# Up projections of a decoder trunk in fp32: four pairs of chunks by seven products instead of eight

## What is computed

```python
D_MODEL, SEQ, DEPTH, D_FF = 1024, 256, 2, 2816
def swiglu_ffn(h, w_in, w_out):
    g, u = jnp.split(h @ w_in, 2, axis=-1)
    return (jax.nn.silu(g) * u) @ w_out
for l in range(DEPTH):
    x = x + 0.5 * swiglu_ffn(rmsnorm(x, norm_ffn1[l]), ffn1_w_in[l], ffn1_w_out[l])
    ...      # four token mixers, then cross attention over mem
    x = x + 0.5 * swiglu_ffn(rmsnorm(x, norm_ffn2[l]), ffn2_w_in[l], ffn2_w_out[l])
return rmsnorm(x, norm_final)
```

## Time and profile before

| | |
|---|---|
| runs of before, median (three runs, 1096.26 to 1097.18) | 1097.18 us |
| the profiled execution, its own time | 1095.27 us |
| its span, first to last instruction | 1093.4 us |
| granted TensorE clock, mean | 0.999 |
| PE, PEld, DVE, ACT, POOL busy share | 99, 83, 75, 53, 36 % |
| hardware queue of SP: bytes, share of 16 engines | 200.55 MB, 55.4 % |

### The profile page before, as it was taken

How to read it: one execution, slowest core, us unless ns; L and a number is a source line. 1 busy time by engine, 2 the same in 40 slices (tenths; PEclk the granted TensorE clock), 3 DMA queues, 4 the chain that set the end, 5 groups by cost and what they waited for, 6 DMA issues and landing times.

```text
span 1093.4 us, 14359 instructions
## 1 busy us (share of the span) xinstructions
PE 1081.8 (99%) x5314; PEld 911.8 (83%) x5314; DVE 820.2 (75%) x1015; ACT 577.0 (53%) x656; POOL 391.8 (36%) x774
## 2 busy tenths in 40 slices
PE   8999999999999999999999999999999999999997
PEld 6888888889898888888878888788988988888886
DVE  6686798799767766668776667878997767666796
ACT  6454454854565544446454444567455555444544
POOL 0687722000000057673226868030000002677800
PEclk9999999999999999999999999999999999999999
DMA  8976557644553477655766764675445436666462
GB/s 277 294 246 215 167 192 256 210 155 149 197 194 116 147 219 225 210 186 182 259 214 209 229 209 150 220 249 193 154 169 187 177 123 197 217 216 217 144 222 107
DMA packets 180722, 215.94 MB, mean 197 GB/s; under 512 B 19088, under 2 KB 138540, under 8 KB 180652
## 3 DMA queue, kind: packets, MB, share of 16 engines
q1 hardware_dynamic: 155324, 200.55, 55.4%
q0 software_dynamic: 24064, 13.16, 4.4%
q10 hardware_dynamic: 1264, 1.32, 0.4%
HBM read 200.79 MB, written 1.05 MB: 185 GB/s over the span
## 4 chain that ended last, share of the span: by engine, by line
PE 88%; DVE 3%; DMA 3%; ACT 2%; issue 1%; POOL 1%; SPq 0%; ACTq 0%; DVEq 0%
PE acc L1640 24%; PE acc L1642 23%; PE acc L1641 23%; PE acc L1656 3%; PE acc L1657 3%; PE acc L1658 3%; PE turn L1517 2%; DMA w_raw<-in_ffn_w_out 2%; ACT w_hi L510 1%; POOL kT L463 1%; DVE w_lo L909 1%; DMA w_raw<-in_ffn_w_in 1%; PE acc L1582 1%; PE acc L1738 1%; PE acc L1737 1%
## 5 line engine op out<-in xcount | busy, mean ns | idle before, releaser
L909 DVE TENSOR_TENSOR w_lo<-w_raw,w_hi 128x2048 fp32r<-128x2048 f32 (+1 forms) x190 | 426.9, 2250 | 165.0 <-ACT w_hi L510 164.3
L510 ACT CAST w_hi<-w_raw 128x2048 fp32r<-128x2048 f32 (+1 forms) x190 | 356.2, 1875 | 195.2 <-PE acc L1642 135.1
L463 POOL DMA_DIRECT2D kT<-kT x704 | 344.3, 498 | 145.7 <-DVE kT L1057 106.8
L1640 PE MATMUL acc<-w_hi,xT 128*128 128x512 f32 x808 | 316.8, 392 | 0.0
L1642 PE MATMUL acc<-w_hi,xT 128*128 128x512 f32 x808 | 314.7, 389 | 0.0
L1641 PE MATMUL acc<-w_lo,xT 128*128 128x512 f32 x808 | 314.4, 389 | 0.0
L1642 PEld LDWEIGHTS acc<-w_hi,xT 128*128 128x128 f32 x808 | 151.7, 188 | 32.0
L1640 PEld LDWEIGHTS acc<-w_hi,xT 128*128 128x128 f32 x808 | 151.7, 188 | 31.1 <-DVE w_lo L909 0.4
L1641 PEld LDWEIGHTS acc<-w_lo,xT 128*128 128x128 f32 x808 | 151.8, 188 | 30.9
L1640 PE MATMUL acc<-w_hi,hT 128*128 128x512 f32 x432 | 170.3, 394 | 1.3 <-DVE w_lo L909 1.2
L1642 PE MATMUL acc<-w_hi,hT 128*128 128x512 f32 x432 | 168.4, 390 | 0.0
(11 more groups left out here) (218 smaller groups left out, 1228.4 us busy)
## 6 DMA issues: line engine op xcount, KB each, us to landing
w_raw<-in_ffn_w_in SPq DMA_DIRECT2D x172, 512.0 KB, 4.8
w_raw<-in_ffn_w_out SPq DMA_DIRECT2D x80, 512.0 KB, 4.4
w_raw<-in_mix_w_in SPq DMA_DIRECT2D x32, 512.0 KB, 4.7
w_raw<-in_xattn_wkv SPq DMA_DIRECT2D x32, 512.0 KB, 4.6
kT<-kT POOLq DMA_DIRECT2D x704, 16.0 KB, 3.4
w_raw<-in_mix_w_out SPq DMA_DIRECT2D x16, 512.0 KB, 4.1
w_raw<-in_xattn_wq SPq DMA_DIRECT2D x16, 512.0 KB, 4.5
w_raw<-in_xattn_wo SPq DMA_DIRECT2D x16, 512.0 KB, 4.3
```

The lines of the kernel that those rows point to most:

```text
L463: pool.dma_start(hfeat[B * q:B * q + B, g % 2, a * RUN:(a + 1) * RUN], hblk[B * a:B * a + B, g % 2, q * RUN:(q + 1) * RUN]).then_inc(hfeat ...
L510: act.copy(w_hi[:, u % SLOTS, 0:n], w_raw[:, u % SLOTS, 0:n]).then_inc(w_split_hi, 1)
L909: dve.tensor_tensor(w_lo[:, u % SLOTS, 0:n], w_raw[:, u % SLOTS, 0:n], w_hi[:, u % SLOTS, 0:n].bitcast(F32), ALU.subtract).then_inc(w_spli ...
L1640: pe.matmul(o, hi, wh, start=((first is True or first == ("tile", t)) and i == 0), stop=False)
```

## The change

In three of the four feed-forward parts (all but the first of layer 0), chunks 2+3, 4+5, 6+7 and 8+9 are computed as pairs. For feature tiles 0 and 1, the two token halves and the two chunks form a 2 x 2 by 2 x 2 block product, which was 8 products and becomes 7: one plain product into `acc` (m1), three of token sums by weight sums, one of a token sum by a plain tile, one of a plain token tile by a weight sum, and one more plain one. Partial results are passed on in PSUM: ScalarE copies m1 to a second bank (`m1_seed`), and copies that bank out twice while it grows (`u2_copy`, `u3_copy`); VectorE adds these copies into the banks of the second chunk (`m5_seed`, `u3_add`). The other 24 products of the pair stay as they are.

The pair's four units hold: u the tiles of features 0 and 1 for both chunks, u + 1 features 2 to 5 of the first chunk, u + 2 features 6 and 7 of both, u + 3 features 2 to 5 of the second. Units u and u + 2 are loaded by four transfers each in place of two. Of unit u only three of four tiles are split; the weight sums (`up_weight_sums`, three subtractions) and their split (`sums_hi`, `sums_lo`) are new. Token sums of features 0 and 1 are made once for each feed-forward part, ahead of `update`. The queues are reordered, and `hidden_hi(9)` in chunk 10 goes behind the second split in all four parts. `k_last` only moves to another place in SBUF.

```diff
+    UP_PAIRS = (2, 4, 6, 8)
+    def paired(l, f, c):
+        return (l, f) != (0, 0) and c in UP_PAIRS
...  ScalarE: split_hi
-                if e and e[0] == "singles":
+                if e and e[0] == "singles" or up_singles(at.l, u)[1]:
                     act.copy(w_hi[:, u % SLOTS, 0:GN], w_raw[:, u % SLOTS, 0:GN])
                     act.copy(w_hi[:, u % SLOTS, 2 * GN:n], w_raw[:, u % SLOTS, 2 * GN:n]).then_inc(w_split_hi, 1)
...  ScalarE: chunk(c)
                         act.activation(gate[:, t, :], acc[c % 3][t][:, 0:HC], ACT.Silu,
                                        scale=rstd[:, V_F2 if f else V_X, t:t + 1]).then_inc(gate_ready, 1)
+                        if t == 0 and paired(l, f, c + 1):
+                            m1_seed(c + 1)
                     if c >= 2:
                         hidden_hi(c - 2)
-                    split_hi(base + 2 * c + 4, at)
+                    if paired(l, f, c + 1):
+                        u2_copy(c + 1)
+                    if not paired(l, f, c) or not paired(l, f, c + 2):
+                        split_hi(base + 2 * c + 4, at)
+                    if paired(l, f, c + 1):
+                        u3_copy(c + 1)
+                    if c == 0 and (l, f) != (0, 0):
+                        up_token_hi()
+                        sums_hi(UP_PAIRS[0])
...
+                    split_hi(base + 2 * c + 5, at)
                     if c == FC - 1:
                         hidden_hi(c - 1)
-                    split_hi(base + 2 * c + 5, at)
+                    if paired(l, f, c + 1) and paired(l, f, c + 3):
+                        split_hi(base + 2 * (c + 3), at)
+                        sums_hi(c + 3)
+                def u3_copy(c):
+                    n = up_pair_no(l, f, c)
+                    act.wait_ge(m7_done, n + 1)
+                    act.copy(u3_sum, acc[c % 3][1][:, :]).then_inc(u3_copied, 1)
...  VectorE: chunk(c), behind the two hact
+                    if paired(l, f, c) and paired(l, f, c + 2):
+                        split_lo(base + 2 * (c + 2), at)
+                    if paired(l, f, c + 1):
+                        m5_seed(c + 1)
                     if c >= 2:
                         hidden_lo(c - 2)
+                    if paired(l, f, c) and paired(l, f, c + 2):
+                        sums_lo(c + 2)
...  behind the transpose
+                    if paired(l, f, c + 1):
+                        first_split()
+                        u3_add(c + 1)
+                        if paired(l, f, c + 3):
+                            up_weight_sums(base + 2 * (c + 3), at)
...  VectorE: ahead of update(b, 1, 0, ...) in boundary (f2in), and at the end of layer 0
+                    if g == G_FFN2:
+                        up_token_sums()
...  TensorE
+                def first_product(c):
+                    u = base + 2 * c
+                    pe.wait_ge(w_split, at0.at(UNITS, SLOTS + u + 1))
+                    plain(acc[c % 3][0][:, :], u, 0, 0, 0, first=True).then_inc(m1_done, 1)
+                def two_chunks(c):
+                    pe.wait_ge(us_ready, 2 * l + f)
+                    pe.wait_ge(ut_split, n + 1)
+                    summed(y1, 0, up_sum(0), first=True)
+                    pe.wait_ge(m1_seeded, n + 1)
+                    summed(x1, 2, up_sum(1)).then_inc(m6_done, 1)
+                    plain(x0, u, 2, 1, 0)
+                    pe.wait_ge(w_split, at0.at(UNITS, SLOTS + u + 2))
+                    plain(x0, u + 1, 0, 2, 0)
+                    pe.wait_ge(u2_copied, n + 1)
+                    summed(x1, 1, up_sum(2)).then_inc(m7_done, 1)
+                    plain(x0, u + 1, 1, 3, 0)
+                    plain(x0, u + 1, 2, 4, 0)
+                    pe.wait_ge(u3_copied, n + 1)
+                    summed(x1, 3, [xT_hi[:, 1, P:2 * P], xT_lo[:, 1, P:2 * P]])
+                    pe.wait_ge(m5_seeded, n + 1)
+                    into(y0, *up_sum(3), w_hi[:, u % SLOTS, 3 * GN:], w_lo[:, u % SLOTS, 3 * GN:]).then_inc(unit_done, 2)
+                    plain(x0, u + 1, 3, 5, 0).then_inc(unit_done, 1)
...
+                    # 4 products of u + 1, then unit u + 2: 4 into x0, x1 and 4 into y0, y1
+                    # (u3_added waited for ahead of y1), then unit u + 3: 4 into y0, the next
+                    # pair's first_product, 4 into y1
```

More of the change, by code:

```diff
@@ L69, in down, with up_singles @@
                 return f, DOWN[u - base]
+        return None, None
+    def up_singles(l, u):
+        for f, base in enumerate((U_F1I, U_F2I)):
+            if base <= u < base + 2 * FC and u % 2 == base % 2 and paired(l, f, (u - base) // 2):
+                return f, (u - base) // 2
         return None, None
@@ L386, in ffn @@
                 at = Layer(l)
+                f = 1 if base == U_F2I else 0
                 for c in range(FC):
+                    if paired(l, f, c):
+                        u = base + 2 * c
+                        pieces = two_chunk_parts(u, src_in, l, 0, c)
+                        unit(u, at, pieces[:2])
+                        for dst, src in pieces[2:]:
+                            sp.dma_start(dst, src).then_inc(second_k_landed, 16)
+                        unit(u + 1, at, pair_parts(u + 1, src_in, l, 2, c * HC, c * HC + FF))
+                        pieces = two_chunk_parts(u + 2, src_in, l, 6, c)
+                        unit(u + 2, at, pieces[:2])
+                        for dst, src in pieces[2:]:
+                            sp.dma_start(dst, src).then_inc(last_k_landed, 16)
+                        unit(u + 3, at, pair_parts(u + 3, src_in, l, 2, (c + 1) * HC, (c + 1) * HC + FF))
+                    if (l, f) != (0, 0) and (c in UP_PAIRS or c - 1 in UP_PAIRS):
+                        continue
                     for j in range(2):
@@ L1047, in first_split @@
                             extra(EXTRA[c])
-                    if c < FC - 1:
+                    if c < FC - 1 and not paired(l, f, c + 1) and not (paired(l, f, c) and paired(l, f, c + 2)):
                         first_split()
@@ L1154, in _ @@
                         xT_lo_part(0, 1, t, at)
[L1155 removed]
+                weights_to(2 if l else 3, at)
                 ffn(l, U_F1I, 0)
@@ L1712, in ffn, with into, plain @@
                 b = 3 if f else 0
+                def into(o, s_hi, s_lo, w_h, w_l, first=False, last=False):
+                    pe.matmul(o, s_hi, w_h, start=first, stop=False, skip_group_check=True)
+                    pe.matmul(o, s_hi, w_l, start=False, stop=False, skip_group_check=True)
+                    return pe.matmul(o, s_lo, w_h, start=False, stop=last, skip_group_check=True)
+                def plain(o, u, at_w, k, t, first=False, last=False):
+                    cols = slice(at_w * GN, (at_w + 1) * GN)
+                    rows = slice(t * P, (t + 1) * P)
+                    return into(o, xT_hi[:, k, rows], xT_lo[:, k, rows], w_hi[:, u % SLOTS, cols], w_lo[:, u % SLOTS, cols], first, last)
@@ new lines, in up_sum, with summed @@
+                def up_sum(i):
+                    return [us_parts[:, i // 2, q, (i % 2) * P:(i % 2 + 1) * P] for q in range(2)]
+                def summed(o, at_w, stationary, first=False):
+                    cols = slice(at_w * GN, (at_w + 1) * GN)
+                    return into(o, *stationary, t_hi[:, cols], t_lo[:, cols], first)
+                def first_product(c):
+                    u = base + 2 * c
+                    pe.wait_ge(w_split, at0.at(UNITS, SLOTS + u + 1))
+                    plain(acc[c % 3][0][:, :], u, 0, 0, 0, first=True).then_inc(m1_done, 1)
@@ L1720, in ffn @@
                 for c in range(1, FC):
+                    if (l, f) != (0, 0) and (c in UP_PAIRS or c - 1 in UP_PAIRS):
+                        if c in UP_PAIRS:
+                            two_chunks(c)
+                        continue
                     if (l, f, c) == (0, 0, 1):
@@ L1724, in ffn @@
                         unit(base + 2 * c, at0, c % 3, xT_hi, xT_lo, 0, True, False)
-                    unit(base + 2 * c + 1, at0, c % 3, xT_hi, xT_lo, GK, False, True)
+                    opens = (l, f) != (0, 0) and c == UP_PAIRS[0] - 1
+                    unit(base + 2 * c + 1, at0, c % 3, xT_hi, xT_lo, GK, False, True,
+                         between=lambda t: first_product(UP_PAIRS[0]) if opens and t == 0 else None)
                     if (l, f) == (0, 0) and c in EXTRA:
```

125 lines of the change are left out of this document (116 added, 9 removed).

## The result

| | before | changed |
|---|---|---|
| median of the runs on one chip | 1097.14 us | 1085.38 us (4 runs, 1084.46 to 1085.74) |
| ratio, 95% interval | | 0.9893 [0.9876, 0.9911] |
| the profiled execution, its own time | 1095.27 us | 1085.74 us |
| its span | 1093.4 us | 1083.9 us |
| granted clock | 0.999 | 0.999 |

The kernel became 11.8 us faster (1.1%), where 8.2 were forecast. In a later set it came to 1085.30 beside 1096.93: 11.6 us. The forecast of 1089.0 is 3.6 too high, and the range, from 1087.5, misses the time on its fast side.

A forecast was written before the change was run, and what follows sets the result against it. PE, busy 99%, was taken as the bound, time being the number of matmuls. -8.16 (products) + 0.94 (token sums) - 1.0 (order) + 0 (added waits) = -8.2 us, from 1097.18 to 1089.0 us; range 1087.5 to 1096.

The forecast's parts named there:

- The products: Up projections: one product of 32 removed in each of 12 pairs, 36 matmuls at 0.2267 us, -8.16 us.
- The relay: m6, copy, m7, copy on ScalarE in each pair: in time, cost 0, with 0.09 us spare at u3_copy.
- the price of a PSUM write: ScalarE's m1_seed taken at 0.59 us, VectorE's adds m5_seed and u3_add at 0.69; bounds 0.4 to 1.2.
- Rival 1: The relay of ScalarE copies in the pairs is late, 0.15 to 0.5 us each: 1091 to 1095, chance 0.25.
- The order: Down projections: hidden_hi(9) behind the second split shortens the split-load-split chain by 0.5 us; -1.0, bounds 0 and -1.5.
- the four waits: PE's waits for VectorE's splits in down projections: 1.2 us shown, about 2.1 us in cost.
- The step from one execution to the median: Whole kernel: the median of before stands 1.91 us over the profiled 1095.27, so -8.2 was taken from 1097.18.
- Token sums: Four 128x128 operations ahead of update: +0.94 us uncovered at the start of layer 1, bounds 0.8 and 1.3.
- VectorE's spare of 2.0 us a pair: VectorE busy 19.1 of 21.08 us; its next u + 1 split due T' + 1.8, T' starting the next pair's products.
- rival 2: VectorE becomes the bound in the pairs, needing 2.7 us more a pair to lose the saving: 1102.5, chance 0.10.
- Rival 3: The removed product turns up as PE waits, 0.5 to 0.7 us a pair: 1095 to 1098, chance 0.10.

The follow-up runs named there:

- the third set: Third set of follow-up timings on one chip, each kernel beside the kernel before: before 1096.93 us, changed kernel 1085.30 us.
- the repeated profile: The kernel before, unchanged, timed and profiled once more: 1096.72 us, ratio 1.0001; profiled execution 1097.38 us, span 1095.5.
- the order-only kernel: Kernel before with only hidden_hi(9) and hidden_lo(9) moved behind the second split: 1094.58 us, ratio 0.9976; later 1093.68, ratio 0.9973.
- the run with one addition: Changed kernel with one more VectorE addition of 1024 columns, result unused, behind sums_lo in every pair: 1093.32 us, ratio 0.9964.
- the old order: Changed kernel with hidden_hi(9) and hidden_lo(9) put back ahead of the second split: 1092.34 us, ratio 0.9957.
- six and nine pairs: Changed kernel with fewer pairs, UP_PAIRS (2, 4) or (2, 4, 6), in place of twelve: six 1091.66 us, nine 1088.10 us.

## Why the prediction missed

The direction and the main term were right, and three terms around it were not. Of the 3.4 us by which the third set (-11.6) went past the -8.2, 2.2 lie in the order (-3.25 against -1.0) and 1.2 in the pairs with their token sums (-8.4 against -7.2).

- **The products, -8.16: right.** 5278 matmuls, pairs 21.08 us apart, no wait in an up projection. By medians of one set the pairs brought 8.4 on top of the order.
- **The relay and the price of a PSUM write: right.** The seed from PSUM to PSUM took 0.57 us (0.59 was taken), VectorE's adds into PSUM 0.694 and 0.693 (0.69 was taken), the copies 0.589 and 0.586. Rival 1 (0.25) didn't happen; its spare of 0.09 measured 0.14.
- **The order, -1.0, bounds 0 and -1.5: the step that failed.** Alone it measured -2.6 and -3.0, and about -7 beside the pairs. The prediction worked out that the four waits cost 2.1 us, found that the moved split heads the chain on which they hang, and then took half of it. The gain on the chain was also sized at 0.5; it is 0.75 and later 1.13, and no wait shows more than 0.7. All of the 2.1 would have had to be taken, and the bound had to reach beyond it, to what a slower execution waits.
- **The step from one execution to the median: failed.** The prediction carried 1.91 us over as if it were fixed. It was for the most part waits of the very kind that the change removes: the repeated profile has 3.4 us of them, not 2.1, at a time 0.7 above its median. Some was the small sample: the medians of before in the three later sets are 0.2 to 0.7 lower than 1097.18. Changed, the profiled execution is 1085.74 and the median 1085.38; no offset is left. With the order at -2.1 the sum is -8.16 + 0.94 - 2.1 = -9.3, and 1095.27 - 9.3 = 1086.0; without the 1.91 on top that is the time within 0.6. That sum is made with the result known.
- **Token sums, +0.94: too high.** Moving them away from the one place that waits brought 0.8 us by the medians of one set and 0.6 by its spans. Part of even that is the wait that the order-only kernel has there without them (0.2 and 0.5).
- **VectorE's spare of 2.0 us a pair (rival 2): wrong, unseen in this kernel.** The down projection's token sums of chunks 0 to 2, which VectorE adds inside `hidden_lo` in the pairs (four operations, 0.93 us), were left out of the count: ahead of the second and third pair of a part the split ends at T' + 1.71, 0.1 ahead of its due time, where 0.8 were thought. Ahead of the fourth, without them, it ends at T' + 0.8, near the T' + 1.0 that was placed (631.37 + 2.25 against T' = 632.84). And rival 2 was said to decide at 2.7 us more a pair, with VectorE's idle time as a buffer; the run with one addition shows that it starts to cost at 0.1 in half of the pairs. The forecast stood because nothing in this kernel came late, not for the reason given.
- **Rival 3** (the product turns up as waits) happened only in the old order, where half of the gain was eaten.

Summed over the third set: -3.25 for the order, -8.4 for the pairs, -11.6 measured; -8.16 for the products and -3.4 for the waits make -11.6 too. But the 3.4 are those of an execution above the median, and the token sums' 0.6 to 0.8 are not in it: the account closes to about 1 us, no better, which is also what the waits drift by between executions and versions. What stays open is why the wait ahead of layer 1 is 1.2 and 1.0 us with six and nine pairs. Which share the two pieces of the new order, ScalarE's and VectorE's, have was not tried.

## What to carry to other kernels

If a change takes away the operation that heads a chain on which waits hang, charge all the waits and bound the gain by them at their full price (the row's idle time plus the part of the matmul that its row hides), and look at several executions, since a profile is one draw: where before differs between runs by waits that the change removes, the difference goes with them. Ask for the spare of a hand-over along the loop from engine to engine and back, in operations between the two signals; VectorE, at 91% of a pair or less by the prediction's count, had 0.1 us to spare in half of them. And time parts of a change both alone and together: here one reordering was worth about 3 us by itself and 7 beside the other half.

## What the runs showed of the hardware

- A wait of PE ahead of a 512-column matmul cost 0.24 us more than its idle time shows (0.46 shown, 0.70 lost): the row ahead of it is 0.39 us long and the step behind it 0.30 (682.71 to 683.01), where two steps would have taken 0.45.
- An idle stretch of 3.34 us (643.16) was followed by 5.7 us of matmuls at a clock of 0.50, another of the same length (988.44) was not; nor were the waits of 0.82 in the kernel with one addition (mean clock 0.999).
- A ScalarE copy that stays in PSUM was no slower than one to SBUF: 570 against 586 and 589 ns. VectorE's add of PSUM and SBUF into PSUM took 694 ns on 512 columns, 10 ns more than the residual update from PSUM into SBUF, 684.
